# Moving waits and weight splits in a one-core, two-network kernel: four places where the engines hand work over

## The chip, the cores and the metric

One core of one Trainium2 chip runs the whole program. The metric is the device time of one execution in microseconds (us). Engines are named as in the profile: PE is TensorE (PEld its weight loads), DVE is VectorE, ACT is ScalarE, POOL is GpSimd, SP is SyncE.

## The reference, cut to what matters

Two networks run one after the other on 256 tokens of width 1024, batch 1, all in float32; `second_block` takes the output of `first_block` as its `x`.

```python
def first_block(x, p, ...):
    h = x
    for i in range(2):                       # an attention mixer, then a feed-forward block, then a gated embedding
        h = h + mixer_i(rms_norm(h, mix_norm[i]))
        ...                                  # relu(h @ w_ff1)**2 @ w_ff2, scaled by the norm
        ...                                  # h + sigmoid(norm(h) @ w_ple_gate) * (p @ w_ple_proj)
    return h

def second_block(x, c, ctx, ...):
    for l in range(DEPTH):
        h_l = _rmsnorm(x, g_pre[l]) * (1.0 + sc_l) + sh_l          # 256 latent tokens
        h_c = _rmsnorm(xc, g_pre[l]) * (1.0 + sc_c) + sh_c         # 256 context tokens
        pl, pc = _split_proj(h_l @ w_in[l]), _split_proj(h_c @ w_in[l])
        ...                                  # softmax attention of latent tokens over latent and context
        gla_l, gla_c = _gla_bidirectional(gla_c_in, gla_l_in)      # chunked linear attention, both directions, 4 heads
        out_l = _mixer_output(pl, att_l, gla_l, *shared)
        ...                                  # the same for the context in the first layer only
        x = x + gt_l * _rmsnorm(out_l, g_post[l])
    return x

def _mixer_output(parts, att_o, gla_o, ...):
    br_a = ((a_b * _short_conv(a_c * a_x, conv_w_l)) * jax.nn.silu(a_z)) @ w_br_conv_l
    br_b = (att_o * jax.nn.silu(z_attn)) @ w_br_attn_l
    br_c = (_rmsnorm(gla_o, gla_g_l) * jax.nn.silu(z_gla)) @ w_br_gla_l
    g_a, g_b, g_c = jnp.split(jax.nn.sigmoid(mg + b_gate_l), 3, axis=-1)
    return (g_a * br_a + g_b * br_b + g_c * br_c) @ w_out_l
```

## The kernel before, in words

Every engine has its own hand-written instruction stream, and semaphores are the only link between them. The order in each stream is the order of the code; nothing is scheduled by a planner.

**Weights.** All weight matrices stream through four slots of a buffer RAW. A quad is four units, one for each slot. For each unit SyncE loads RAW (line 410); ScalarE rounds it to a high part WHI (`hi_unit`, line 470); VectorE subtracts to get the low part WLO (`lo`, line 963, called `lo(n)` for n units); TensorE then computes three products for one float32 product: high by high, high by low, low by high (`product`, lines 1970 to 1972). TensorE waits for a unit's low part (`unit`) before it uses the slot. ScalarE may overwrite a slot's WHI only when TensorE has finished with it (`gemm_step`). So each `lo` in VectorE's stream stands between TensorE and its next unit, and where it stands among VectorE's other work is chosen by hand.

**Gate of the first network's second layer.** `segment("gate1", ...)` on ScalarE and the loop at line 1451 on VectorE handle two blocks of four units. In the same stage the second network's context rows CTX are loaded (1 MB), ScalarE squares them (`x_squares(1)`), VectorE turns the sums into a scale and a diagonal matrix (`x_scale(1)`), adds the modulation biases, and signals `x_diag`; TensorE transposes and scales the context with it (`turn_x(1)`, line 2208) after the first unit of the second block. MASK is a table of level masks used later.

**Linear attention (gla).** Four heads in each of the two layers. Per head TensorE computes eight rounds of scores (`gla_scores(0)` to `gla_scores(7)`, line 2422). VectorE prepares the operands of most rounds (`gla_level(n)`, lines 1567 and 1574; scores(7) needs level(6)) and copies each result by mask (`gla_place(m)`, line 1583). `gla_values` (line 2464) needs place(7). Then VectorE squares, takes roots and scales rows (`gla_squares`, `gla_roots`, `gla_rows`, lines 1607 to 1621), TensorE transposes the rows (`gla_rows`, line 2471), and VectorE multiplies by gains (`gla_gains`, line 1627, which signals `g_normed`). `columns(q, u, half)` are twelve weight products of a gate projection that TensorE does between these steps. Layer 0 works on 512 tokens, layer 1 on 256 (only the latent ones), so its rows are half as wide.

**Gated branch behind it (mgc).** `gated` runs two blocks of products of ATH, whose results ScalarE turns into sigmoids (`sigmoid_g`, line 835, which frees the banks), and then two blocks of products of BTH. Meanwhile `gate_z(0)` and `gate_z(1)` on VectorE multiply (line 1701), combine (line 1694) and split (lines 1479 and 1481, signals `bt_ready`) the operand BTH. The second sigmoid room shares memory with a tile that `gate_z(1)` reads at line 1701.

**Value projection of the softmax attention (v).** `rows_product` on TensorE does four units with the query sums and one rotation product (`rotated`, line 2576) between them; VectorE runs `query_scales` (which ends in `rotate(0)`, lines 1765 to 1768, and waits for the rotation product) and copies four banks to VA (line 1830, which frees them). TensorE then does one gate unit, waits for the four banks, and starts the scores (line 2635).

Of the kernel before, what the change touches and what calls it, by code (L numbers as in the profile page):

```python
# [8 lines left out]
ALU = mybir.AluOpType  # L9
# [6 lines left out]
S = 256  # L16
# [4 lines left out]
SLOTS = 4  # L21
# [158 lines left out]
def mixer_kernel(nc, io, out):  # L180
# [3 lines left out]
    with ExitStack() as ctx:  # L184
# [195 lines left out]
        o_done, o_squared, g_bc, g_bcast = (sem(n) for n in ("o_done", "o_squared", "g_bc", "g_bcast"))  # L380
        sig_done, bt_ready, inputs_ready, z_read = sem("sig_done"), sem("bt_ready"), sem("inputs_ready"), sem("z_read")
        tri_in, tri_ready = sem("tri_in"), sem("tri_ready")
# [75 lines left out]
        def _(act):  # L458
# [143 lines left out]
            for layer in range(2):  # L602
# [64 lines left out]
                if layer:  # L667
                    act.wait_ge(ada_taken, 2)
                    act.drain()
                    act.dma_start(CTX, io["ctx_2"][0].rearrange("(t p) n -> p t n", p=P)).then_inc(ctx_in, 16)  # L670

                    def context_squares(base):
                        act.wait_ge(ctx_in, 16)
                        act.dma_start(MASK, io["mask"]).then_inc(mask_in, 16)
                        x_squares(1)

                    segment(f"gate{layer}", [2, 2], sigmoid, {(0, 0, 0): context_squares, (0, 1, 0): lambda base: x_affine(0, 1)})
                    act.wait_ge(h_ready, T.next(h_ready, 2))
                    x_squares(0)
                else:  # L680
                    segment(f"gate{layer}", [2, 2], sigmoid, {(0, 1, 2): lambda base: norm_chunks("mix_norm", 1, (0, 1))})
# [8 lines left out]
            for layer in range(2):  # L690
# [135 lines left out]
                def sigmoid_g(b, rooms=G):  # L826
                    def work(j, base):
                        if j == 1 and b == 2:
                            act.wait_ge(z_read, layer + 1)
                        if j < 2 and b == 1:  # L830
# [119 lines left out]
        def _(dve):  # L950
# [394 lines left out]
            for layer in range(2):  # L1345
# [86 lines left out]
                if layer:  # L1432
                    lo(1)
                    x_scale(1)
# [16 lines left out]
                for b in range(2):  # L1451
# [4 lines left out]
                    else:  # L1456
                        lo(SLOTS - 2 - layer)
                        if b:
# [42 lines left out]
            for layer in range(2):  # L1501
# [175 lines left out]
                gla_level(5, GH - 1)  # L1677
                lo(1)
                gla_place(5)
                gla_place(6)  # L1680
                gla_level(6, GH - 1)
                gla_place(7)
# [14 lines left out]
                def gate_z(i):  # L1697
                    w = SIGZ[:, i * 4 * TOK:(i + 1) * 4 * TOK].rearrange("p (c n) -> p c n", c=4)[:, :, 0:tq]
                    for c in range(4):
                        dve.wait_ge(sig_done, T.next(sig_done))  # L1700
                        last = V.tensor_tensor(w[:, c, :], w[:, c, :], ZRAW[4 * i + c][:, 0:tq], ALU.mult)
                        if i == 1 and c == 3:
                            last.then_inc(z_read, 1)
                        if c % 2:
# [121 lines left out]
                lo(1)  # L1826
                query_scales()
                for c in range(TT):
                    dve.wait_ge(gemm_step, base + TT * (SLOTS - 1) + c + 1)
                    freed(V.tensor_copy(VA[:, c, :], bank[c][:, 0:AKV * AD]), c)  # L1830
                lo(SLOTS - 1)
                T.next(gemm_step, TT * SLOTS)
# [129 lines left out]
        def _(pe):  # L1962
# [353 lines left out]
            for layer in range(2):  # L2316
# [228 lines left out]
                gla_last(i)  # L2545
                gla_scores(6, i)
                columns(GH, 2, 0)
                gla_scores(7, i)
                columns(GH, 2, 1)
                gla_values(i)  # L2550
                columns(GH, 3, 0)
                columns(GH, 3, 1)
                gla_rows()
                T.next(g_normed)
                pe.wait_ge(*outside(GH, 3))
# [44 lines left out]
                def key_scales_first():  # L2600
# [7 lines left out]
                rows_product(AKV * AD, after={0: lambda: query_sums(4, 5), 1: lambda: query_sums(6, 7),  # L2608
                                              2: lambda: rotated(bank[6][:, 0:S], QS[:, 0, 0:S])})

# [199 lines left out]
```

## Time and profile before

| | us |
|---|---|
| median of three executions | 2278.73 |
| lowest, highest | 2278.49, 2279.85 |
| the profiled execution | 2279.85 |
| its span, first to last instruction | 2278.1 |
| mean granted TensorE clock | 0.991 |

The times are device times of whole executions; the span lies inside the profiled one. The granted clock is the share of full speed that TensorE was given, on average over the span.

### The profile page before, as it was taken

Reading aid. Unit: us, or ns where it says so; the run is one execution under the profiler, and the core shown is the slowest. Engines: PE = TensorE matmul, PEld = TensorE weight load, DVE = VectorE, ACT = ScalarE, POOL = GpSimd, SP = SyncE. Lnnn points to the kernel's source line nnn. Section 1 sums busy time; section 2 is a strip of 40 time slices with the busy share of each in tenths; the row PEclk is TensorE's granted clock in tenths of the full one; section 3 lists DMA queues with packets and bytes.
Section 4 is the critical chain, followed back from the end, with each engine's and each line's share of the span. In section 5 each row is a group of like instructions: output and inputs, shape, how many; then the busy total and the mean of one; then the engine's idle time right before and its main releaser. Section 6 shows DMA issues by size and latency. Waiting matters only on the chain.

```text
span 2278.1 us, 34052 instructions
## 1 busy us (share of the span) xinstructions
PE 2210.5 (97%) x13330; PEld 1954.7 (86%) x13330; DVE 1506.9 (66%) x2751; ACT 978.1 (43%) x1627; POOL 34.2 (2%) x37
## 2 busy tenths in 40 slices
PE   8899999999999999999999999999999999999998
PEld 6689988878998989988888888888888999979997
DVE  6879888778988567755346443643565766566665
ACT  5564445475445554432225422223235444354342
POOL 0000000000000011000000000000000100000000
PEclk9999999999999999999999999999999999999999
DMA  5347774526876411122331233333223124425653
GB/s 191 102 135 239 252 231 157 185 67 218 268 232 196 133 47 38 39 68 85 93 83 33 74 107 98 95 97 98 91 67 93 47 77 147 116 80 159 184 178 109
DMA packets 189670, 285.14 MB, mean 125 GB/s; under 512 B 9476, under 2 KB 83332, under 8 KB 189256
## 3 DMA queue, kind: packets, MB, share of 16 engines
q1 hardware_dynamic: 187264, 276.60, 39.2%
q10 hardware_dynamic: 2248, 6.38, 0.8%
q8 instruction: 106, 1.74, 0.3%
q14 instruction: 52, 0.43, 0.1%
HBM read 281.89 MB, written 1.05 MB: 124 GB/s over the span
## 4 chain that ended last, share of the span: by engine, by line
PE 81%; DVE 10%; DVEq 3%; ACT 3%; issue 2%; DMA 1%; ACTq 0%; SPq 0%
PE bank L1970 23%; PE bank L1971 22%; PE bank L1972 22%; DVE WLO L963 2%; PE bank L2422 2%; PE bank L2635 1%; PE bank L2659 1%; PE bank L2361 1%; PE bank L2362 1%; DMA RAW<-in_e_w_in 1%; PE bank L2457 1%; ACT WHI L470 1%; PE bank L2444 1%; PE bank L2367 1%; PE bank L2161 1%
## 5 line engine op out<-in xcount | busy, mean ns | idle before, releaser
L963 DVE TENSOR_TENSOR WLO<-RAW,WHI 128x1024 fp32r<-128x1024 f32 (+2 forms) x500 | 581.7, 1171 | 450.1 <-ACT WHI L470 440.3
L470 ACT ACTIVATE WHI<-RAW 128x1024 fp32r<-128x1024 f32 (+2 forms) x500 | 506.5, 1017 | 849.2 <-PE bank L1972 816.5
L1970 PE MATMUL bank<-ATH,WHI 128*128 128x256 f32 (+1 forms) x2032 | 664.3, 327 | 8.2 <-DVE h L1018 1.8
L1972 PE MATMUL bank<-ATH,WLO 128*128 128x256 f32 (+1 forms) x2032 | 651.8, 321 | 0.0
L1971 PE MATMUL bank<-ATL,WHI 128*128 128x256 f32 (+1 forms) x2032 | 651.8, 321 | 0.0
L1970 PEld LDWEIGHTS bank<-ATH,WHI 128*128 128x128 f32 x2032 | 386.7, 190 | 41.8 <-DVE WLO L963 3.9
L1971 PEld LDWEIGHTS bank<-ATL,WHI 128*128 128x128 f32 x2032 | 386.9, 190 | 28.4 <-issue 0.7
L1972 PEld LDWEIGHTS bank<-ATH,WLO 128*128 128x128 f32 x2032 | 386.5, 190 | 28.5
L1970 PE MATMUL bank<-WHI,ATH 128*128 128x512 f32 (+2 forms) x996 | 358.2, 360 | 9.5 <-DVE WLO L963 6.3
L1971 PE MATMUL bank<-WLO,ATH 128*128 128x512 f32 (+2 forms) x996 | 353.7, 355 | 0.0
L1972 PE MATMUL bank<-WHI,ATL 128*128 128x512 f32 (+2 forms) x996 | 353.2, 355 | 0.0
L1970 PEld LDWEIGHTS bank<-WHI,ATH 128*128 128x128 f32 x996 | 189.5, 190 | 39.8 <-issue 7.4
L1972 PEld LDWEIGHTS bank<-WHI,ATL 128*128 128x128 f32 x996 | 189.7, 190 | 26.5
L1971 PEld LDWEIGHTS bank<-WLO,ATH 128*128 128x128 f32 x996 | 189.8, 191 | 25.1
L1970 PE MATMUL bank<-BTH,WHI 128*128 128x512 f32 (+1 forms) x384 | 129.9, 338 | 0.5
L1971 PE MATMUL bank<-BTL,WHI 128*128 128x512 f32 (+1 forms) x384 | 129.0, 336 | 0.0
L1972 PE MATMUL bank<-BTH,WLO 128*128 128x512 f32 (+1 forms) x384 | 129.0, 336 | 0.0
L1374 DVE SCALAR_TENSOR_TENSOR ARENA<-ARENA,CTMP 128x384 f32<-128x384 f32 x224 | 127.8, 612 | 0.1
L1970 PEld LDWEIGHTS bank<-BTH,WHI 128*128 128x128 f32 x384 | 72.8, 190 | 9.6 <-DVE ARENA L1734 1.7
L1972 PEld LDWEIGHTS bank<-BTH,WLO 128*128 128x128 f32 x384 | 72.8, 190 | 7.5
L1971 PEld LDWEIGHTS bank<-BTL,WHI 128*128 128x128 f32 x384 | 72.8, 190 | 7.5
L2361 PE MATMUL bank<-BTH,BTL 128*128 128x256 f32 (+1 forms) x256 | 68.3, 301 | 3.7 <-DVE BTL L1549 3.1
(298 smaller groups left out, 2412.8 us busy)
## 6 DMA issues: line engine op xcount, KB each, us to landing
RAW<-in_w_in SPq DMA_DIRECT2D x192, 512.0 KB, 3.6
RAW<-in_w_ff SPq DMA_DIRECT2D x128, 512.0 KB, 4.6
ARENA<-in_w_ada SPq DMA_DIRECT2D x64, 384.0 KB, 4.8
RAW<-in_o_w_in SPq DMA_DIRECT2D x24, 512.0 KB, 3.9
RAW<-in_e_w_in SPq DMA_DIRECT2D x16, 512.0 KB, 5.1
RAW<-in_w_ple_gate SPq DMA_DIRECT2D x16, 512.0 KB, 3.8
RAW<-in_w_br_gla SPq DMA_DIRECT2D x16, 512.0 KB, 3.5
RAW<-in_w_br_attn SPq DMA_DIRECT2D x16, 512.0 KB, 3.5
```

The lines of the kernel that those rows point to most:

```text
L470: nc.scalar.activation(WHI[:, slot, 0:n], RAW[:, slot, 0:n], ACT.Copy).then_inc(hi_split, 1)
L963: V.tensor_tensor(WLO[:, slot, 0:n], RAW[:, slot, 0:n], WHI[:, slot, 0:n], ALU.subtract).then_inc(lo_split, 1)
L1374: V.scalar_tensor_tensor(a, w, s, a, ALU.mult, ALU.add)
L1970: mm(o, ah, bh, start=start, stop=False, skip_group_check=free)
L1971: mm(o, ah, bl, start=False, stop=False, skip_group_check=free)
L1972: return mm(o, al, bh, start=False, stop=stop, skip_group_check=free)
L2161: mm(bank[3][:, S + 2 * n + v:S + 2 * n + v + 1], ACC[v][:, at:at + P], cst("ones")[:, 0:1], start=False, stop=False, skip_group_check=True)
L2361: mm(o, LAS[i % 2][:, 0, d, t, :], columns, start=True, stop=False)
L2362: return mm(o, LAS[i % 2][:, 1, d, t, :], columns, start=False, stop=True)
L2367: last = mm(bank[b0 + d][:, t * P:(t + 1) * P], RA[:, t * P:(t + 1) * P], WD[:, d, bass.ds(i * GDK, GDK)], start=True, stop=True)
L2422: last = mm(bank[4 + m % 2][:, tk], key, q, start=True, stop=True)
L2444: last = mm(room, P1[:, 0, d, t * P:(t + 1) * P], v[t], start=True, stop=True)
```

## The change

Nothing is computed differently. Waits, splits and products change place at four points:

- In the gate of the second layer, ScalarE issues the MASK transfer right behind the CTX transfer and does the context squares ahead of the segment; VectorE does `x_scale(1)` and the modulation ahead of the second block's first `lo`.
- In the last head of the linear attention, VectorE's `lo(1)` moves behind place(5) and place(6); TensorE does scores(7) and the values ahead of the last column products of slot 2; after the transposes TensorE waits for `g_normed`.
- The semaphore `z_read` is gone; ScalarE's second sigmoid block waits for `bt_ready` of `gate_z(1)`.
- In the value projection, two `lo` move ahead of the four copies, and the rotation product moves from behind unit 2 to behind unit 3.

```diff
-                    def context_squares(base):
-                        act.wait_ge(ctx_in, 16)
-                        act.dma_start(MASK, io["mask"]).then_inc(mask_in, 16)
-                        x_squares(1)
-
-                    segment(f"gate{layer}", [2, 2], sigmoid, {(0, 0, 0): context_squares, (0, 1, 0): lambda base: x_affine(0, 1)})
+                    act.dma_start(MASK, io["mask"]).then_inc(mask_in, 16)
+                    act.wait_ge(ctx_in, 16)
+                    x_squares(1)
+                    segment(f"gate{layer}", [2, 2], sigmoid, {(0, 1, 0): lambda base: x_affine(0, 1)})
...
                         if j == 1 and b == 2:
-                            act.wait_ge(z_read, layer + 1)
+                            act.wait_ge(bt_ready, layer * 10 + 2)
...
                 if layer:
-                    lo(1)
                     x_scale(1)
...
                     else:
-                        lo(SLOTS - 2 - layer)
+                        lo(SLOTS - 2)
...
                 gla_level(5, GH - 1)
-                lo(1)
                 gla_place(5)
                 gla_place(6)
+                lo(1)
                 gla_level(6, GH - 1)
...
-                        last = V.tensor_tensor(w[:, c, :], w[:, c, :], ZRAW[4 * i + c][:, 0:tq], ALU.mult)
-                        if i == 1 and c == 3:
-                            last.then_inc(z_read, 1)
+                        V.tensor_tensor(w[:, c, :], w[:, c, :], ZRAW[4 * i + c][:, 0:tq], ALU.mult)
...
                 query_scales()
+                lo(SLOTS - 2)
                 for c in range(TT):
                     dve.wait_ge(gemm_step, base + TT * (SLOTS - 1) + c + 1)
                     freed(V.tensor_copy(VA[:, c, :], bank[c][:, 0:AKV * AD]), c)
-                lo(SLOTS - 1)
+                lo(1)
...
                 gla_scores(6, i)
+                gla_scores(7, i)
+                gla_values(i)
                 columns(GH, 2, 0)
-                gla_scores(7, i)
                 columns(GH, 2, 1)
-                gla_values(i)
                 columns(GH, 3, 0)
                 columns(GH, 3, 1)
                 gla_rows()
-                T.next(g_normed)
+                pe.wait_ge(g_normed, T.next(g_normed))
                 pe.wait_ge(*outside(GH, 3))
...
                 rows_product(AKV * AD, after={0: lambda: query_sums(4, 5), 1: lambda: query_sums(6, 7),
-                                              2: lambda: rotated(bank[6][:, 0:S], QS[:, 0, 0:S])})
+                                              3: lambda: rotated(bank[6][:, 0:S], QS[:, 0, 0:S])})
```

## Rows read from the trace of the kernel before

**Rows 1.** The page, part 1: busy us, share of span, instructions, by engine.

```profile
PE 2210.5 (97%) x13330; PEld 1954.7 (86%) x13330; DVE 1506.9 (66%) x2751; ACT 978.1 (43%) x1627; POOL 34.2 (2%) x37
```

**Rows 2.** Timeline, gate stage: start, duration, engine line op, count [idle before <-releaser].

```profile
733.79 0.17 DVE L1326 TENSOR_SCALAR STAT<-STAT 128x2 f32<-128x2 f32 x1 [1.68 <-ACT ARENA L656]
...
738.77 2.28 DVE L963 TENSOR_TENSOR WLO<-RAW,WHI 128x1024 fp32r<-128x1024 f32 x2
...
737.79 0.39 PE L1970 MATMUL bank<-WHI,ATH 128*128 128x512 f32 x1
```

**Rows 3.** DMA issues, gate stage: tensor, queue, count, size, us to landing.

```profile
ARENA<-in_ctx ACTq DMA_DIRECT2D x1, 1024.0 KB, 6.0
```

**Rows 4.** Timeline, last head of layer 0 (862.04: the gains of an earlier head).

```profile
862.04 1.40 DVE L1627 TENSOR_SCALAR ARENA<-bank,COL 128x512 f32<-128x512 f32 x2
...
997.77 0.74 DVE L1567 SCALAR_TENSOR_TENSOR ARENA<-ARENA 128x256 f32<-128x256 f32 x2
1000.59 0.74 DVE L1583 COPY_PREDICATED ARENA<-ARENA,bank 128x512 f32<-128x512 int32 x1 [2.09 <-issue]
...
995.74 1.14 PE L2422 MATMUL bank<-ARENA 128*128 128x128 f32 x8
996.63 0.48 PE L1970 MATMUL bank<-ATH,WHI 128*128 128x512 f32 x1
...
999.49 1.06 PE L2422 MATMUL bank<-ARENA 128*128 128x128 f32 x8
...
1012.67 1.97 PE L2471 MATMUL bank<-CST,ARENA 128*128 128x128 f32 x8 [2.21 <-DVE ARENA L1621]
```

**Rows 5.** Timeline, last head of layer 1.

```profile
1878.59 0.48 DVE L1567 SCALAR_TENSOR_TENSOR ARENA<-ARENA 128x128 f32<-128x128 f32 x2
...
1876.48 0.36 PE L1970 MATMUL bank<-ATH,WHI 128*128 128x256 f32 x1
...
1879.13 0.71 PE L2422 MATMUL bank<-ARENA 128*128 128x128 f32 x4 [0.98 <-DVE ARENA L1567]
...
1887.71 0.66 PE L2471 MATMUL bank<-CST,ARENA 128*128 128x128 f32 x4 [2.71 <-DVE ARENA L1621]
```

**Rows 6.** Timeline, gated branch of layers 0 and 1: split, sigmoid, first BTH product.

```profile
1057.20 2.29 DVE L1481 TENSOR_TENSOR BTL<-ARENA,BTH 128x2048 fp32r<-128x2048 f32 x1
...
1054.91 0.69 ACT L835 ACTIVATE ARENA<-bank,COL 128x512 f32<-128x512 f32 x1 [0.36 <-PE bank L1972]
...
1058.73 0.39 PE L1970 MATMUL bank<-BTH,WHI 128*128 128x512 f32 x1
...
1911.73 1.22 DVE L1481 TENSOR_TENSOR BTL<-ARENA,BTH 128x1024 fp32r<-128x1024 f32 x1
...
1909.52 0.95 ACT L835 ACTIVATE ARENA<-bank,COL 128x256 f32<-128x256 f32 x2
...
1911.24 0.28 PE L1970 MATMUL bank<-BTH,WHI 128*128 128x256 f32 x1
```

**Rows 7.** Timeline, value projection of layer 1: rotate, copies, splits; gate unit, scores.

```profile
1986.59 0.42 DVE L1765 TENSOR_TENSOR SPARE<-CST,bank 128x256 f32<-128x256 f32 x1 [0.19 <-PE bank L2576]
...
1987.77 0.75 DVE L1830 COPY ARENA<-bank 128x256 f32<-128x256 f32 x2
...
1989.81 3.48 DVE L963 TENSOR_TENSOR WLO<-RAW,WHI 128x1024 fp32r<-128x1024 f32 x3
...
1989.26 0.28 PE L1970 MATMUL bank<-ATH,WHI 128*128 128x256 f32 x1
...
1992.14 1.88 PE L2635 MATMUL bank<-ARENA 128*128 128x512 f32 x4
```

**Rows 8.** Windows behind long idles: stretch; length, PE busy; PEclk, DMA share, GB/s.

```profile
86.00:91.00 5.00, 4.12 (x27) 1.00 0.01 3
1012.00:1017.00 5.00, 4.33 (x16) 0.66 0.37 105
...
1888.00:1893.00 5.00, 5.00 (x45) 1.00 0.55 136
```

More of the change, by code:

```diff
@@ L380, in mixer_kernel @@
         o_done, o_squared, g_bc, g_bcast = (sem(n) for n in ("o_done", "o_squared", "g_bc", "g_bcast"))
-        sig_done, bt_ready, inputs_ready, z_read = sem("sig_done"), sem("bt_ready"), sem("inputs_ready"), sem("z_read")
+        sig_done, bt_ready, inputs_ready = sem("sig_done"), sem("bt_ready"), sem("inputs_ready")
         tri_in, tri_ready = sem("tri_in"), sem("tri_ready")
```

## The prediction

> **What bounds the kernel now.** I read the page first. TensorE is busy for 2210.5 of 2278.1 us [rows 1], so all its idle time together is 67.6 us. Nothing in this change shortens or removes a product, so it can only move that idle time: at best it gives back a few waits, at worst it makes new ones. Therefore I read, at each of the places that the diff touches, the timeline of TensorE, VectorE and ScalarE, and asked two questions: when does TensorE want the thing, and when does the new order deliver it. Last I looked at the granted clock behind TensorE's longer idles. In rows 2, 4, 5, 6 and 7 the reader should compare the start of a PE row with the end (start plus duration) of the DVE or ACT row that releases it. A line of "lo" (L963) is the split of one weight unit: 1.14 us from start to start (2.28 us for two, [rows 2]).
>
> **Part 1, the gate of the first network's second layer (ScalarE lines 667 to 679, VectorE lines 1432 to 1457).** Before, VectorE split the first unit of the second gate block ahead of x_scale(1). Now x_scale(1), the modulation sums, a drain and a memset come first, and the split after them. x_scale starts at 733.79, held by ScalarE's squares, and that start does not get earlier: the squares wait for the context rows from memory both before and after the change. So the chain ends where it did, at 738.77, and the split that now stands there is the first unit's [rows 2]. It ends at about 739.95, and TensorE, which opened that block at 737.79, opens it at 740.05. Cost 2.3 us. ScalarE's own reordering (squares ahead of one high split) delays that high split to 734.7, which is before 738.77 and hidden; if that cover were gone it would cost at most the 1.05 us of one high split. The lo split that falls due next, of unit two, still ends before TensorE's first unit is through. What follows in the stage (turned context, key products) hangs on TensorE, so the 2.3 us stay. The mask transfer, moved right behind the context transfer, costs nothing if it queues behind it; the context took 6.0 us to land [rows 3], and how the mask could lengthen that is a rival below.
>
> **Part 2, the last head of the linear attention, in both layers (VectorE line 1678, TensorE lines 2547 to 2554).** Three edits act together. TensorE no longer puts column products between scores(6), scores(7) and the values; VectorE's split moves from before place(5) to between place(6) and level(6); and TensorE now waits for g_normed after the transposes.
>
> Layer 0 [rows 4]: scores(6) starts at 995.74 and TensorE is free at 996.63. A place follows the start of its scores by 1.10 us (999.49 to 1000.59), so place(6) runs from 996.84 and the moved split from 997.5. level(6), which began at 997.77, begins at 998.6 and ends at 999.4. scores(7) needs it: idle 2.8 us. It holds TensorE 0.8 us; place(7) begins 1.10 us after scores(7) and lasts 0.75 us, so values wait until 1001.3: idle 1.1 us. Then four column halves of about 2.8 us cover VectorE's squares, roots and rows (7.6 us), and the 2.21 us idle before the transposes [rows 4] goes. Behind the transposes is the new wait: VectorE can start its two gains when half of the transposes are done, about 0.7 us after their start, and they take 1.40 us together [rows 4]; the transposes hold TensorE 0.8 us, so idle 1.4 us (1.3 to 1.5). The product queued behind it is the first of the next stage, and everything else of TensorE waits with it. The old idle was followed by a stretch at half clock, worth 1.7 us [rows 8], which I also take off. Sum: 2.8 + 1.1 + 1.4 - 2.2 - 1.7 = +1.4 us.
>
> Layer 1 [rows 5], by the same steps with half the columns: level(6) ended at 1879.07; now place(6) starts at 1876.8 (scores(6) start 0.45 us before TensorE is free, and a place follows the narrower scores by 0.76), the split at 1877.2, and level(6) ends at 1878.8. TensorE is free at 1876.5: idle 2.4 us where 1.0 us (0.98) stood behind one column half. Idle before the values 0.8 us. The products then end at 1886.7, when VectorE's rows end too, so the 2.71 us go. But VectorE's queue there holds a split of 1.14 us ahead of the gains, so the g_normed wait is 1.5 us. Sum: 2.4 + 0.8 + 1.5 - 1.0 - 2.7 = +1.0 us. Bounds for both layers together: 0 (lags shorter by 0.3 us at each of eight hand-overs) to 5 us.
>
> **Part 3, z_read replaced by the split's semaphore (lines 829 and 1701 to 1703).** ScalarE's four sigmoids of the second gate block waited for VectorE's last multiply; they now wait for the split, three VectorE steps and one weight unit later. The sigmoids free the banks that TensorE's next block (the BTH products) writes. In layer 0 the split ends at 1059.49 (1057.20 + 2.29); the first sigmoid, 0.69 us, ends at 1060.25, and TensorE wants the bank at 1058.73 [rows 6]: idle 1.5 to 1.6 us. In layer 1 the split ends at 1912.95, one sigmoid takes 0.48 us (two in 0.95), TensorE wants the bank at 1911.24 [rows 6]: idle 2.3 us. The other three banks follow faster than TensorE asks. Queued behind the waiting sigmoid on ScalarE is the high split of slot 3, which TensorE wants three units later: hidden. VectorE's split is itself paced by TensorE's previous unit, so an earlier delay does not open slack here. Cost 3.9 us.
>
> **Part 4, the value projection of the softmax attention (lines 1826 to 1831 and 2608).** The rotation product moves behind the last unit, so VectorE's rotate starts 3.06 us later (the unit's length), and two splits now stand ahead of the four copies that free banks 0 to 3. Layer 1 [rows 7]: TensorE opens the gate unit at 1989.26; rotate starts about 0.4 us behind that, at 1989.65 instead of 1986.59, and lasts 1.18; two splits 2.28 (three took 3.48 with the drain of the last), copies 0.34 apart (0.75 for two), the last ends at 1994.55. TensorE is through its gate unit at 1992.14, when it started the scores: idle 2.4 us. The next rotation was late by 0.35 us before and needs the third split and a gain; it comes out 2.3 us later, so 2.3 us is the cost. Bounds 1.5 to 2.8. In layer 0 the same VectorE queue is 4.9 us long, against two halves of 2.8 us of wider products (996.63 to 999.49, [rows 4]): hidden by 0.1 us or more; without that cover it would cost the same 2.3 us. No wait existed at the old place of the rotation, so nothing is gained by the move.
>
> **The sum.** 2.3 + 1.4 + 1.0 + 3.9 + 2.3 = 10.9 us, without the clock.
>
> **The clock.** Apart from the first 13 us, TensorE had five idles of 1.9 us or more (before 85.19, 1012.67, 1731.84, 1748.56 and 1887.71). In the 5 us behind three of them the granted clock averaged 0.66 (it stood at 0.50, the 1.2 GHz level, for part of them); behind the first and the last it stayed at 1.00, 2.4 GHz [rows 8]. So one fall costs 5 x 0.34 = 1.7 us of product time. The change makes five idles of 2.3 to 2.8 us (parts 1, 2 twice, 3 and 4, layer 1) and four or five of 0.8 to 1.6 us. With three in five, three falls: 5.1 us. None to six is possible: 0 to 10 us. The Trainium skill ("TensorE: Matmul & The Clock Gate", part 1) says that the monitor's window runs free and does not start anew with a kernel; by that, which of two like idles is followed by a fall depends on where it happens to lie. The three of five here agree.
>
> The profiled execution took 2279.85 us (span 2278.1), the highest of three; the median is 2278.73. 2279.85 + 10.9 + 5.1 = 2295.9 for that execution, and the same 16 us on the median give 2294.7. I say 2295.
>
> **The rivals.** *The waits come, but the clock does not fall behind them:* 2278.7 + 10.9 = 2289.6. For it: the 2.71 us idle had no fall. *The mask transfer lengthens the context transfer:* if the two shared the engines by bytes (1024 KB in 6.0 us, [rows 3]; the mask is half as many), the context would land up to 3.0 us later, and the squares, x_scale and TensorE's wait with it: 2298. Against it: one queue issues both, in order. The Trainium skill ("DMA: Bandwidth & Descriptors", Issuing engines are not separate DMA queues) says that transfers of all issuers interleave on the same engines; by it the sharing is with SyncE's weights in either order, and the mask only adds. *Parts 3 and 4 are covered after all*, because VectorE's work ahead of the split or the copies can start earlier than I read: the sum falls to 10.9 - 6.2 = 4.7, without falls, 2283, the border of no change. *Faster:* TensorE has queued enough behind a wait that waits under some 2.5 us do not idle it, while the removed 2.21 and 2.71 us and their fall are real. Then -6.6 us: 2272. It decides at an idle of about 2.5 us; against it stands the 0.98 us idle of [rows 5], released by VectorE and plainly seen on TensorE.
>
> **How the numbers follow.** The forecast with one to five falls 0.62; no fall 0.16; mask 0.09; covered 0.09; faster 0.04. A measurement here can tell 0.2%, 4.6 us, from no change. Slower by over 0.2%: the first three cases and a bit of the fourth, 0.89; within 0.2%: 0.07; faster: 0.04. Range for 8 in 10: from 10.9 less a hidden part of 2.3 and no fall, 2287, to six falls with a fuller mask delay, 10.9 + 10 + 2 = 23, 2302. I give 2286 to 2302.
>
> **What would show it.** After: an idle of 2.3 us on TensorE at 740 behind a VectorE lo split; two idles ahead of the last scores and the values in each layer and none ahead of the transposes; an idle ahead of the first product of the next stage released by the gains; an idle of 1.5 and 2.3 us ahead of the first BTH products, released by ScalarE's sigmoid; 2.4 us ahead of the first softmax scores in layer 1 and nothing in layer 0. Wrong would be: VectorE reaching the first unit's split before 736, or TensorE's busy time growing by more than five falls explain.

## The result, and the profile after

The changed kernel took 2298.77 us (median of 4 runs, 2298.19 to 2299.74), the kernel before 2279.29 us on the same chip (median of 4). The ratio is 1.0085, with a 95% interval of 1.0073 to 1.0097: slower by 19.5 us. The forecast was 2295 us and slower; its range was 2286 to 2302. All 18 executions of the changed kernel have a median of 2298.30 us and range over 2295.43 to 2303.16, so no single execution tells a microsecond.

The profiled execution of the changed kernel took 2300.87 us with a span of 2299.1 us, 21.0 us more than that of before. I read its views in the order of the prediction. Line numbers in its rows are up to 6 lower than in the rows of before (the split of a weight unit is L960, the products L1965 to L1967). First part 1 of the page, as in [rows 1]:

```profile
PE 2224.7 (97%) x13330; PEld 1964.9 (85%) x13330; DVE 1506.9 (66%) x2751; ACT 977.1 (42%) x1627; POOL 34.2 (1%) x37
```

VectorE and ScalarE did the same work in the same time. TensorE did the same number of products, but its busy time grew by 14.2 us: products at half clock last about twice as long (scores(7) below). So the page alone says that a good part of the difference is the clock, and not waiting. Some 5 us of it, though, lie ahead of 725, where both kernels are the same; about 9 us lie behind.

**The gate stage.** The timeline answers to [rows 2], the DMA issues to [rows 3]:

```profile
727.18 0.39 ACTq L670 DMA_DIRECT2D ARENA<-in_ctx  x1
...
735.04 1.06 ACT L656 ACTIVATE ARENA<-ARENA 128x1024 f32<-128x1024 f32 x1 [7.93 <-DMA ARENA<-in_ctx]
...
737.27 0.17 DVE L1323 TENSOR_SCALAR STAT<-STAT 128x2 f32<-128x2 f32 x1 [4.49 <-ACT ARENA L656]
...
742.23 3.42 DVE L960 TENSOR_TENSOR WLO<-RAW,WHI 128x1024 fp32r<-128x1024 f32 x3
...
743.44 0.50 PE L1965 MATMUL bank<-WHI,ATH 128*128 128x512 f32 x1 [3.32 <-DVE WLO L960]
```

```profile
ARENA<-in_ctx ACTq DMA_DIRECT2D x1, 1024.0 KB, 7.8
```

Of before, the issue of the context and the first squares:

```profile
725.00 0.39 ACTq L670 DMA_DIRECT2D ARENA<-in_ctx  x1
...
731.57 1.06 ACT L656 ACTIVATE ARENA<-ARENA 128x1024 f32<-128x1024 f32 x1 [0.71 <-DMA ARENA<-in_ctx]
```

Read the rows of after from the bottom: TensorE waits 3.32 us for a low part. That split is the first of three which VectorE starts at 742.23, and it could not start sooner because x_scale (737.27) waited for ScalarE's squares, and those for the context. The chain is the predicted one, about 1 us longer, because ScalarE's squares started 7.9 us after the issue of the context (727.18 to 735.04) and not 6.6 (725.00 to 731.57 before). The context landed 1.8 us later; 0.6 us of that came back, because before ScalarE issued the mask between the landing and the squares.

**The last head of the linear attention**, layer 0 and then layer 1, against [rows 4] and [rows 5]:

```profile
1004.40 0.75 DVE L1563 SCALAR_TENSOR_TENSOR ARENA<-ARENA 128x256 f32<-128x256 f32 x2
...
1005.21 2.07 PE L2417 MATMUL bank<-ARENA 128*128 128x128 f32 x8 [2.59 <-DVE ARENA L1563]
...
1008.10 3.74 PE L2459 MATMUL bank<-ARENA 128*128 128x256 f32 x8 [0.82 <-DVE ARENA L1579]
...
1022.59 1.03 PE L2466 MATMUL bank<-CST,ARENA 128*128 128x128 f32 x8
...
1024.69 0.50 PE L1965 MATMUL bank<-ATH,WHI 128*128 128x512 f32 x1 [1.07 <-DVE ARENA L1623]
...
1888.95 1.22 PE L2417 MATMUL bank<-ARENA 128*128 128x128 f32 x4 [2.06 <-DVE ARENA L1563]
...
1890.71 2.08 PE L2459 MATMUL bank<-ARENA 128*128 128x256 f32 x4 [0.54 <-DVE ARENA L1579]
...
1899.71 0.60 PE L2466 MATMUL bank<-CST,ARENA 128*128 128x128 f32 x4
...
1901.07 0.39 PE L1965 MATMUL bank<-ATH,WHI 128*128 128x256 f32 x1 [0.75 <-DVE ARENA L1623]
```

In each layer there are two idles ahead of scores(7) and the values, none ahead of the transposes, and one ahead of the next stage's first product, released by the gains. The six sum to 7.83 us; the three of before that are gone summed to 5.90 us (2.21, 0.98, 2.71). Net 1.93 us. Look also at the durations: scores(7) take 2.07 us in layer 0 where they took 1.06 [rows 4]. They run at half clock.

**The gated branch** of layers 0 and 1 [rows 6], and **the value projection** of layer 1 [rows 7]:

```profile
1069.15 2.42 ACT L832 ACTIVATE ARENA<-bank,COL 128x512 f32<-128x512 f32 x4 [4.97 <-DVE BTL L1477]
...
1069.99 0.47 PE L1965 MATMUL bank<-BTH,WHI 128*128 128x512 f32 x1 [1.47 <-ACT ARENA L832]
...
1925.96 1.57 ACT L832 ACTIVATE ARENA<-bank,COL 128x256 f32<-128x256 f32 x4 [3.38 <-DVE BTL L1477]
...
1926.58 0.55 PE L1965 MATMUL bank<-BTH,WHI 128*128 128x256 f32 x1 [2.22 <-ACT ARENA L832]
...
2006.33 0.42 DVE L1759 TENSOR_TENSOR SPARE<-CST,bank 128x256 f32<-128x256 f32 x1 [3.07 <-PE bank L2571]
...
2007.51 2.35 DVE L960 TENSOR_TENSOR WLO<-RAW,WHI 128x1024 fp32r<-128x1024 f32 x2
...
2009.78 1.41 DVE L1825 COPY ARENA<-bank 128x256 f32<-128x256 f32 x4
...
2011.45 3.44 PE L2630 MATMUL bank<-ARENA 128*128 128x512 f32 x4 [2.28 <-DVE ARENA L1825]
```

Idles of 1.47, 2.22 and 2.28 us, each with the releaser that was named. In layer 0 the value projection shows no idle of over 0.3 us.

**The clock.** Windows behind the idles, to compare with [rows 8]; the columns are length, PE busy, PEclk, DMA share, GB/s:

```profile
743.00:748.00 5.00, 4.56 (x28) 1.00 0.68 209
1004.00:1009.00 5.00, 2.97 (x10) 0.58 0.37 105
1009.00:1014.00 5.00, 5.00 (x18) 0.73 0.01 3
1888.00:1893.00 5.00, 3.51 (x10) 0.59 0.38 108
1893.00:1898.00 5.00, 5.00 (x34) 0.73 0.01 2
1926.00:1931.00 5.00, 4.42 (x25) 0.66 0.18 60
2011.00:2016.00 5.00, 4.55 (x12) 0.66 0.97 273
```

A "fall" is a stretch in which the granted clock stands at 0.50, the 1.2 GHz level. A fall costs 5 x 0.34 = 1.7 us, as before. Behind 1004 and behind 1888 two windows in a row are low: 5 x 0.42 + 5 x 0.27 = 3.4 us, and 3.4 us, two falls without a break. I added up (1 - granted clock) over windows of 1 us for the whole span: 20.0 us before, 32.7 us after. Every stretch that was not cut by the end of the span came to 1.7 us or a multiple. Two falls of the difference lie ahead of 725, where both kernels are the same; five lie behind 740, where before had three and after has eight.

In these two profiles, from 740 to the end, the bill is: idles 3.32 + 1.93 + 3.69 + 2.28 = 11.2 us; five falls 8.5 us; less 1.5 us, because one old idle of 1.93 us (before 1731.84) is only 0.44 us after (a section below tells why). Sum 18.2 of the 18.8 us by which the two profiles drift apart there (21.0 at the end, 2.2 at 725).

### The profile page after: what moved, and what is told of

It reads as the page before. It is cut to its first block, busy times and chain, and to the rows that moved or that the text cites. A ratio compares the mean times of both kernels' runs of the same rounds, so it can differ in the third digit from the quotient of the medians.

```text
span 2299.1 us, 34054 instructions
## 1 busy us (share of the span) xinstructions
PE 2224.7 (97%) x13330; PEld 1964.9 (85%) x13330; DVE 1506.9 (66%) x2751; ACT 977.1 (42%) x1627; POOL 34.2 (1%) x37
## 4 chain that ended last, share of the span: by engine, by line
PE 78%; DVE 12%; ACT 3%; DVEq 3%; issue 3%; DMA 1%; ACTq 0%; SPq 0%
PE bank L1965 22%; PE bank L1966 21%; PE bank L1967 21%; DVE WLO L960 3%; PE bank L2417 1%; PE bank L2630 1%; PE bank L2654 1%; ACT WHI L470 1%; DMA RAW<-in_e_w_in 1%; PE bank L2356 1%; PE bank L2452 1%; PE bank L2357 1%; PE bank L2439 1%; PE bank L2362 1%; DVEq L1374 1%
## 5 line engine op out<-in xcount | busy, mean ns | idle before, releaser
L960 DVE TENSOR_TENSOR WLO<-RAW,WHI 128x1024 fp32r<-128x1024 f32 (+2 forms) x500 | 581.8, 1171 | 454.5 <-ACT WHI L470 444.8
L1965 PE MATMUL bank<-ATH,WHI 128*128 128x256 f32 (+1 forms) x2032 | 665.0, 327 | 9.9 <-DVE ARENA L1623 1.8
L1967 PE MATMUL bank<-ATH,WLO 128*128 128x256 f32 (+1 forms) x2032 | 652.3, 321 | 0.0
L1965 PEld LDWEIGHTS bank<-ATH,WHI 128*128 128x128 f32 x2032 | 387.5, 191 | 44.2 <-DVE WLO L960 3.8
L1967 PEld LDWEIGHTS bank<-ATH,WLO 128*128 128x128 f32 x2032 | 387.3, 191 | 28.4
L1965 PE MATMUL bank<-WHI,ATH 128*128 128x512 f32 (+2 forms) x996 | 358.6, 360 | 12.3 <-DVE WLO L960 9.0
L1967 PE MATMUL bank<-WHI,ATL 128*128 128x512 f32 (+2 forms) x996 | 354.0, 355 | 0.0
L1965 PEld LDWEIGHTS bank<-WHI,ATH 128*128 128x128 f32 x996 | 190.3, 191 | 42.9 <-DVE WLO L960 10.1
L1967 PEld LDWEIGHTS bank<-WHI,ATL 128*128 128x128 f32 x996 | 190.1, 191 | 26.6
L1965 PE MATMUL bank<-BTH,WHI 128*128 128x512 f32 (+1 forms) x384 | 130.7, 340 | 4.2 <-ACT ARENA L832 3.7
L1967 PE MATMUL bank<-BTH,WLO 128*128 128x512 f32 (+1 forms) x384 | 129.6, 337 | 0.0
L1965 PEld LDWEIGHTS bank<-BTH,WHI 128*128 128x128 f32 x384 | 73.5, 191 | 13.8 <-issue 4.2
L1967 PEld LDWEIGHTS bank<-BTH,WLO 128*128 128x128 f32 x384 | 73.5, 191 | 7.5
```

The lines of the kernel that those rows point to most:

```text
L960: V.tensor_tensor(WLO[:, slot, 0:n], RAW[:, slot, 0:n], WHI[:, slot, 0:n], ALU.subtract).then_inc(lo_split, 1)
L1965: mm(o, ah, bh, start=start, stop=False, skip_group_check=free)
L1967: return mm(o, al, bh, start=False, stop=stop, skip_group_check=free)
```

## The experiments

Twelve kernels, each the kernel before with the edit named or shown. Times are medians; "before" is the kernel before on the same chip. The repeats of the kernel before ranged over 2275.67 to 2285.54 us, so an interval is about 0.1%, some 2 us, to either side.

A profile shows the falls of one execution only. But the mean granted clock of every execution is known, and (1 - granted clock) x span is what that execution lost to the clock. Below, "lost to the clock" is this loss, averaged over all executions of a kernel, less the same for before on that chip, with a 95% interval.

### The four parts one by one

Edits: the hunks of the diff for the gate stage (gate_only), for the last head (tail_only), for `z_read` (branch_only) and for the value projection (value_only).

> The kernel before with part 1 alone (gate of the first network's second layer). Theory: TensorE idles about 3.3 us at the second gate block, as in the changed kernel, and nothing else moves: +3.3 us at an unchanged clock, +5.0 with one more fall. Rival: the idle is taken back later, because what waits behind it has slack: +0 to +1 us.

> The kernel before with part 2 alone (last head of the linear attention in both layers). Theory: the idles of the changed kernel (2.6, 0.8, 1.1 and 2.1, 0.5, 0.8 us) less those of before (2.2; 1.0, 2.7): +1.9 us of idle, and each group of idles is followed by two clock falls where before had one in both layers together: 3 x 1.7 = 5.1 more, +7.0 us. Rival: the falls there are a matter of the execution, not of the part; then +1.9 us.

> The kernel before with part 3 alone (ScalarE's second sigmoid block waits for the split). Theory: idles of 1.5 and 2.2 us ahead of the first products of the split operand: +3.7 us, +5.4 with the fall that followed the second one in the changed kernel. Rival: the delay is hidden when nothing else is late before it: under +1 us.

> The kernel before with part 4 alone (value projection of the softmax attention). Theory: one idle of 2.3 us in layer 1, none in layer 0: +2.3 us, +4.0 with the fall that followed it. Rival: under +1 us, the next rotation was late anyway. If the four parts add up, their sum is +19.5 us; a sum near 11 says that the rest is a matter of the parts together.

Against before at 2279.51 us:

| | us | ratio (95%) | slower by | idle added, own profile | rest | lost to the clock |
|---|---|---|---|---|---|---|
| gate_only | 2282.94 | 1.0012 (1.0002 to 1.0022) | 3.4 | 2.4 | 1.0 | 0.1 +- 2.1 |
| tail_only | 2286.17 | 1.0030 (1.0019 to 1.0042) | 6.7 | 1.9 | 4.8 | 5.1 +- 2.3 |
| branch_only | 2284.35 | 1.0023 (1.0013 to 1.0033) | 4.8 | 3.7 | 1.1 | -0.4 +- 2.3 |
| value_only | 2283.07 | 1.0015 (1.0006 to 1.0023) | 3.6 | 2.3 | 1.3 | 0.5 +- 1.4 |
| sum | | | 18.5 | 10.3 | 8.2 | 5.3 |

The parts add up to 18.5 us, where the whole change made 19.5. Within the intervals they are independent, and no wait is taken back by slack behind it. Three parts cost their idle; the rest of 1.0 to 1.3 us each is smaller than its interval, and the clocks of their executions do not show it. The last head is the exception: 1.9 us of idle and 4.8 us more, and 5.1 us lost to the clock. Its profile shows why, with 8 us windows (the other engines' busy times stand between):

```profile
998.00:1006.00 8.00, 5.47 (x17) 4.53 (x18) 2.37 (x5) 0.00 (x0) 0.00 (x0) 0.57 0.22 68
1882.00:1890.00 8.00, 6.87 (x28) 6.22 (x29) 3.90 (x19) 0.00 (x0) 0.00 (x0) 0.57 0.22 68
```

8 x 0.43 = 3.4 us: two falls in each layer, as in the changed kernel. The six idles are 2.59, 0.82, 1.07, 2.06, 0.54 and 0.75 us, the same as there to 0.01 us. The rows of scores(6) and scores(7) in both layers are needed below:

```profile
995.98 1.14 PE L2422 MATMUL bank<-ARENA 128*128 128x128 f32 x8
...
999.71 2.08 PE L2422 MATMUL bank<-ARENA 128*128 128x128 f32 x8 [2.59 <-DVE ARENA L1567]
...
1879.85 0.69 PE L2422 MATMUL bank<-ARENA 128*128 128x128 f32 x4
...
1882.60 0.89 PE L2422 MATMUL bank<-ARENA 128*128 128x128 f32 x4 [2.06 <-DVE ARENA L1567]
```

### The gate stage: transfer or split?

mask_only moves the transfer alone, gate_split_only moves VectorE's split alone:

```diff
                     act.dma_start(CTX, io["ctx_2"][0].rearrange("(t p) n -> p t n", p=P)).then_inc(ctx_in, 16)
+                    act.dma_start(MASK, io["mask"]).then_inc(mask_in, 16)
                     def context_squares(base):
                         act.wait_ge(ctx_in, 16)
-                        act.dma_start(MASK, io["mask"]).then_inc(mask_in, 16)
```

```diff
                 if layer:
-                    lo(1)
                     x_scale(1)
...
-                        lo(SLOTS - 2 - layer)
+                        lo(SLOTS - 2)
```

> The kernel before with the MASK transfer alone issued right behind the CTX transfer; squares and splits stay where they were. Theory: nothing, 0 +- 0.5 us: the context lands 6.0 to 7.5 us after its issue whether the mask is behind it or not (6.0, 6.0, 6.8 and 7.5 us in four traces with the mask at its old place, 6.8 and 7.8 in two with it at the new). Rival: the mask shares the transfer's bandwidth; the context lands 7 to 9 us after its issue and TensorE waits for the modulation at the second gate block: +0.5 to +1.5 us.

> The kernel before with VectorE's half of part 1 alone (x_scale(1) and the modulation ahead of the first split); ScalarE and both transfers as before. Theory: this order alone makes the idle: 2.3 us or a little more where the context lands late, +2.3 to +3.4 us. Rival: ScalarE's order (squares ahead of a high split) is what holds TensorE; then under +1 us here.

mask_only: 2279.38 us against 2279.57, ratio 0.9999 (0.9991 to 1.0008). No cost, though in its profile the context took 7.5 us to land. In eleven traces with the mask in its old place the context took 6.0 to 7.5 us, with a mean of 6.8; in three with the mask right behind it 6.8, 7.5 and 7.8. The 7.8 of the changed kernel's profile is probably mostly that scatter; whether the mask adds some tenths stays open, and the time shows nothing of it. The move even helps a little where the context is late: with a landing of 7.5 us, value_only and vlo_only, with the mask in its old place, have an idle of 0.84 and 0.76 us at the gate, released by the modulation (L1439), and mask_only has 0.25 us. The issue of the mask, 0.6 us, no longer stands between the landing and the squares. (The 0.84 us are not in the table above; they come and go with the landing.)

gate_split_only: 2283.66 us, ratio 1.0017 (1.0006 to 1.0028), +4.1 us. VectorE's order alone makes the idle:

```profile
741.20 3.42 DVE L963 TENSOR_TENSOR WLO<-RAW,WHI 128x1024 fp32r<-128x1024 f32 x3
...
742.41 0.50 PE L1969 MATMUL bank<-WHI,ATH 128*128 128x512 f32 x1 [2.90 <-DVE WLO L963]
```

It costs as much as the whole part 1, within the intervals. ScalarE's new order and the transfer add nothing that can be told.

### The value projection: each half alone

```diff
                 query_scales()
+                lo(SLOTS - 2)
                 for c in range(TT):
...
-                lo(SLOTS - 1)
+                lo(1)
```

```diff
-                                              2: lambda: rotated(bank[6][:, 0:S], QS[:, 0, 0:S])})
+                                              3: lambda: rotated(bank[6][:, 0:S], QS[:, 0, 0:S])})
```

> The kernel before with one half of part 4: two splits ahead of the four copies, the rotation product at its old place. Theory: the copies end at about 1990.8 on the time scale of before (1987.77 + 2.28 + 0.75), TensorE wants the banks at 1992.14: no idle, 0 +- 0.5 us. Rival: the splits alone make the 2.3 us idle.

> The kernel before with the other half of part 4: the rotation product behind unit 3, VectorE's queue as before. Theory: the rotate ends 3.06 us later, at about 1990.8, the copies at 1991.6, TensorE wants the banks at 1992.14: no idle there, 0 to +0.5 us. If both halves alone cost nothing, the 2.3 us of part 4 come from the two together. Rival: the late rotation alone costs 2 us, at the scores or at the next rotation.

vlo_only: 2279.52 us, ratio 1.0001 (0.9992 to 1.0009). rot_only: 2281.01 us, ratio 1.0008 (0.9999 to 1.0017). The rows, of vlo_only, rot_only and value_only in turn:

```profile
1985.27 1.41 DVE L1831 COPY ARENA<-bank 128x256 f32<-128x256 f32 x4
```

```profile
1990.55 1.41 DVE L1830 COPY ARENA<-bank 128x256 f32<-128x256 f32 x4
...
1995.87 0.70 PE L2576 MATMUL bank<-ARENA,CST 128*128 128x256 f32 x2 [1.70 <-DVE ARENA L1760]
```

```profile
1990.54 3.05 PE L2636 MATMUL bank<-ARENA 128*128 128x512 f32 x4 [2.28 <-DVE ARENA L1831]
```

Neither half alone has an idle ahead of the scores (line 2635 in before); only both together have. I had expected nothing at all from rot_only. There the scores start on time, but the next rotation product then waits 1.70 us: VectorE prepares its operand (L1760) behind the copies and three splits, all 3 us late. The median is 1.4 us higher, which the interval can't tell from nothing.

### The last head: the wait alone, the order alone

norm_only replaces `T.next(g_normed)` by the wait. order_only makes this move on TensorE:

```diff
                 gla_scores(6, i)
+                gla_scores(7, i)
+                gla_values(i)
                 columns(GH, 2, 0)
-                gla_scores(7, i)
                 columns(GH, 2, 1)
-                gla_values(i)
```

> The kernel before with the wait for g_normed alone (behind the transposes of the last head). Theory: it adds the idles of the changed kernel there, 1.07 and 0.75 us, and takes none away: +1.8 us; the 2.2 and 2.7 us ahead of the transposes stay. Rival: what follows the transposes waits for something as late as the gains anyway: under +0.5 us.

> The kernel before with TensorE's order of part 2 alone (scores(7) and the values ahead of the column products of slot 2); VectorE's split and the missing wait as before. Theory: idles of 2.0 and 0.8 us in layer 0 for the 2.2 that go, and of 2.3 and 0.5 in layer 1 for 1.0 and 2.7: -0.2 us, that is no change, and one or two more clock falls at most, +3.4. Rival: the order alone makes the loss of part 2, +5 us or more.

norm_only: 2285.52 us against 2279.13, ratio 1.0026 (1.0016 to 1.0036): +6.4 us where 1.8 were expected. The new idles are a little longer than in the changed kernel, and the old ones ahead of the transposes (2.20 and 2.72 us) stay:

```profile
1012.75 1.09 PE L2471 MATMUL bank<-CST,ARENA 128*128 128x128 f32 x8 [2.20 <-DVE ARENA L1621]
...
1015.20 0.50 PE L1970 MATMUL bank<-ATH,WHI 128*128 128x512 f32 x1 [1.36 <-DVE ARENA L1627]
...
1889.71 0.58 PE L1970 MATMUL bank<-ATH,WHI 128*128 128x256 f32 x1 [1.26 <-DVE ARENA L1627]
```

1.36 + 1.26 = 2.6 us. The other 3.8 us of the median are not in this profile: it is of the fastest of the eight executions (2282.97 us, granted clock 0.991) and has one fall at these two places, behind 1889, as other traces of kernels without the wait have. The other seven executions had granted clocks of 0.987 to 0.989, and the eight together lost 5.3 +- 2.1 us more to the clock than before. So the rest is falls; at which places they lie no profile shows. The one profile also has two idles close together in each layer (2.20 and 1.36 us, 2.72 and 1.26 us), with no fall behind the first pair and one behind the second.

order_only: 2283.27 us, ratio 1.0021 (1.0012 to 1.0029), +4.1 us. Its idles sum to less than those of before (1.67 + 0.82 + 2.41 + 0.54 = 5.44 us, against 5.90), and yet it is slower:

```profile
998.53 2.07 PE L2422 MATMUL bank<-ARENA 128*128 128x128 f32 x8 [1.67 <-DVE ARENA L1567]
...
1001.43 2.93 PE L2464 MATMUL bank<-ARENA 128*128 128x256 f32 x6 [0.82 <-DVE ARENA L1583]
```

```profile
998.00:1006.00 8.00, 6.65 (x20) 0.57 0.14 51
1879.00:1887.00 8.00, 6.64 (x29) 0.57 0.24 68
```

Here the loss is the clock alone: 3.4 us in each layer, 6.8 in all, where the profile of before lost 1.7 at its transposes. -0.5 + 5.1 = +4.6 us, and 4.1 were measured. Over all twelve executions 6.6 +- 1.3 us more were lost to the clock, so this is no accident of the profile. The theory had the idles right and its "one or two more falls at most" was one too low; its rival, that the order alone makes the loss, was nearer.

norm_only and order_only do not add up to tail_only: 6.4 + 4.1 us against 6.7, because norm_only keeps the idles ahead of the transposes, which the new order removes. VectorE's moved split was not run alone; by the rows it makes the first idle of layer 0 longer (2.59 against 1.67 us) and that of layer 1 shorter (2.06 against 2.41 us).

### A better order

If scores(7) and the values are only moved as far as their operands are ready, the idle ahead of the transposes can go without a new long one. one_half moves the values over one column half; half_and_split also moves the split:

```diff
                 gla_scores(7, i)
+                gla_values(i)
                 columns(GH, 2, 1)
-                gla_values(i)
```

```diff
                 gla_level(5, GH - 1)
-                lo(1)
                 gla_place(5)
                 gla_place(6)
                 gla_level(6, GH - 1)
                 gla_place(7)
+                lo(1)
```

> The kernel before with one move on TensorE: the values of the last head come ahead of the second column half of slot 2, so that three halves stand between them and the transposes. Theory: layer 0 idles 0.8 us ahead of the values and not at the transposes (before 2.2), layer 1 0.5 us there and 1.4 at the transposes (before 2.7): -2.2 us, and up to two clock falls fewer, -2 to -5 us. Rival: an idle of under 1 us costs a fall as readily as one of over 2 us; then no change.

> As one_half, and VectorE's split moves from ahead of place(5) to behind place(7), where VectorE waits for the values. Theory: layer 0 as one_half; in layer 1 level(6) is ready 1.1 us earlier and the 1.0 us ahead of scores(7) goes: -3.2 us of idle in all, with falls -3 to -6 us. Rival: the later split is late for the column products of slot 3, or delays the squares by as much as it gives: no better than one_half.

one_half: 2276.76 us, ratio 0.9991 (0.9982 to 1.0000). half_and_split: 2275.41 us, ratio 0.9983 (0.9975 to 0.9992), 3.7 us faster than before. The rows of half_and_split:

```profile
1002.60 1.99 PE L2464 MATMUL bank<-ARENA 128*128 128x256 f32 x8 [0.82 <-DVE ARENA L1583]
...
1876.32 0.60 PE L2422 MATMUL bank<-ARENA 128*128 128x128 f32 x4
...
1877.31 1.22 DVE L963 TENSOR_TENSOR WLO<-RAW,WHI 128x1024 fp32r<-128x1024 f32 x1
...
1877.46 1.13 PE L2464 MATMUL bank<-ARENA 128*128 128x256 f32 x4 [0.54 <-DVE ARENA L1583]
...
1884.17 0.66 PE L2471 MATMUL bank<-CST,ARENA 128*128 128x128 f32 x4 [1.28 <-DVE ARENA L1621]
```

The 0.98 us ahead of scores(7) is gone (1876.32 has no idle), the split runs while TensorE does the values, and 0.82 + 0.54 + 1.28 = 2.64 us stand for 5.90: -3.3 us. Neither layer of this trace has a fall here. The executions of both kernels lost as much to the clock as those of before (0.3 +- 1.7 us for one_half, 0.0 +- 1.5 for half_and_split), so the 3.7 us are idle alone, within the interval; no fewer falls are shown. The second step over one_half (1.4 us by the medians) is about as large as its idle says (1.0 us), but the two intervals overlap.

## Why the prediction was right, point by point

**Part 1, 2.3 us.** Right in mechanism and place; 2.4 us of idle in gate_only, 2.9 in gate_split_only, 3.3 in the changed kernel's profile. What sets its length is the time from the issue of the context to ScalarE's squares: 6.90, 7.45 and 7.86 us in these three gave idles of 2.37, 2.90 and 3.32 us, one for one. That time scatters with the landing (6.0 to 7.8 us in fourteen traces; the working used one of 6.0, the shortest), and it holds 0.6 us for the issue of the mask only where the mask is issued behind the landing, as in gate_split_only. The mask rival had the time almost exactly (2298 us), and by the time alone could not be told from the forecast. It is refuted by its mechanism: the context landed 1.8 us later and not 3.0, the idle was 3.3 us, and moving the mask alone changes nothing. The Trainium skill ("DMA: Bandwidth & Descriptors", Issuing engines are not separate DMA queues) has the transfers of all issuers interleave on the same engines. The scatter of 6.0 to 7.5 us with the mask elsewhere is in keeping with that; no run here shows it directly.

**Part 2, +1.4 and +1.0 us.** The six idles were put at 2.8, 1.1, 1.4, 2.4, 0.8 and 1.5 us, and are 2.59, 0.82, 1.07, 2.06, 0.54 and 0.75: all where they were said to be, each 0.2 to 0.75 us shorter. The hand-overs themselves were right: from the start of scores(6) to that of scores(7) the working had 3.66 and 2.77 us, and tail_only took 3.73 and 2.75 (999.71 less 995.98, 1882.60 less 1879.85). But the working let TensorE be free 0.89 and 0.45 us after the start of scores(6), where the next product used to start. With nothing queued behind, scores(6) count as busy for 1.14 and 0.69 us. So about 0.25 us ahead of scores(7) is lost overlap of two products, which the idle does not count but the time does. The same holds for scores(7) and the transposes of layer 0: the working had them hold TensorE for 0.8 us, and they count as busy for 1.06 [rows 4] and 1.03. The last idle of layer 1 is truly shorter: the gains wait less behind VectorE's split. This makes 1.9 us without the clock where the working had 1.4 + 1.7 + 1.0 = 4.1. But the part costs 6.7 us. The term that was mis-sized is the clock here: I gave each long idle three chances in five of one fall. Scores(7) behind their idle, and the values behind theirs of 0.5 to 0.8 us, had two falls each time.

**Part 3, 3.9 us.** 1.47 and 2.22 us, sum 3.7; branch_only 4.8 us. Nothing was covered.

**Part 4, 2.3 us.** 2.28 us; value_only 3.6. The two halves make the idle only together, as the sum by rows says (two splits and 3 us of rotation, each of which fits alone). What I had not priced is that the late rotation has a price of its own at the next rotation product, which shows when the splits do not already hold up TensorE.

**The clock, three falls, 5.1 us, less one taken off in part 2.** Between the two profiles it is five more from 740 on, 8.5 us; over many executions (18 of the changed kernel, mean granted clock 0.9867, against 91 of before, 0.9906) 9.0 +- 1.2 us more were lost to the clock. The prediction's net was 5.1 - 1.7 = 3.4 us: too low by 5 to 6. Nearly all of that is the last head: its share of the prediction was two long idles x 0.6 x 1.7 - 1.7 = 0.3 us, and tail_only lost 5.1. The idles without clock were set at 12.6 and are 10.3 to 11.2. So the total of +16 for +19.5 comes of two errors of opposite sign: idles 1.4 to 2.3 us too long, falls 5 us too few. That it came within 4 us is in part luck.

**The rivals.** Waits without falls (2289.6) is refuted by the clock rows and by the time. Parts 3 and 4 covered: refuted by branch_only and value_only. Faster, because short waits do not idle TensorE: refuted by every row above. My test for a wrong forecast, that TensorE's busy time should not grow by more than five falls explain (8.5 us), was badly drawn: it grew by 14.2 us, but some 5 us of that lie ahead of the change's first edit, where this execution had two falls more; the 9 us behind are what five falls explain.

## What to carry to other kernels

Moving an operation ahead on the busy engine gains only as far as its operand is ready: of two engines that hand work back and forth, count the other's queue up to the operand, and leave just enough independent work between. Price an idle of TensorE at its length, and look at the granted clock over many executions for the rest: in the last head the clock cost more than the idle that was added, in the other three parts it cost nothing that can be told. In a kernel that is 97% busy on one engine, undo the parts one by one with many repeats: parts of 3 us were told from nothing only because each ran 6 to 12 times.

## What the runs showed of the hardware

**Idles repeat, falls do not.** The same idle of TensorE has the same length to 0.02 us in every trace (2.21, 2.71, 2.06 us), but the granted clock behind it falls in some only. Over the fourteen traces: behind the 2.21 us idle of layer 0 in 3 of 9, behind the 2.71 us idle in 4 of 9, behind the 2.06 us idle near 1748 in 12 of 14, behind the 1.93 us idle near 1732 in 5 of 7, behind the lone new ones of 2.2 to 3.3 us in 4 of 7. Together 28 of 46, 0.61, where the prediction took three in five. (Two of the 46, those of norm_only, have a second idle close behind.) Length says little: the longest, 3.32 us, had none. The Trainium skill ("TensorE: Matmul & The Clock Gate", What's actually happening) says that the monitor's window runs free, so that the point of a transition shifts from run to run. These counts agree. The scatter of the unchanged kernel over 10 us is in part this: over its 91 executions the time rose with what was lost to the clock (correlation 0.62), but only by some 0.3 to 0.5 us for each us lost.

**In the last head, two falls.** Where scores(7) and the values each waited within 3 us of each other, with 1.67 to 2.59 us and then 0.54 to 0.82 us, all 6 cases in three kernels (the changed one, tail_only, order_only) lost 3.4 us, two falls in one stretch at 1.2 GHz. The same short idles with nothing longer than 1.0 us ahead of them (0.82 and 0.54 us in one_half and half_and_split, four cases) had no fall. That two idles close together are the cause is not shown: the two pairs of norm_only, around the transposes, had no fall and one. What else is special to scores(7) and the values was not tested.

**A fall ahead of an idle is mostly paid by it.** The idle near 1732 is 1.93 us in seven traces and 0.42 to 0.52 us in the other seven; these are just the seven in which the clock fell between 1717 and the idle. The row of the changed kernel, whose clock is low from 1731:

```profile
1743.21 0.39 PE L2356 MATMUL bank<-BTH,BTL 128*128 128x256 f32 x1 [0.44 <-DVE BTL L1545]
```

TensorE arrives 1.5 us later at something that was not ready anyway. So of a fall's 1.7 us only 0.2 remain there. This is one reason why the time rises by less than what the clock loses.
